# Stick-breaking attention with two heads per step and running sums over later keys, and one block of the top-k selection moved into attention A

## What is computed

```python
# branch B: stick-breaking attention, 8 heads of width 64, strictly causal
z = einsum('bqhd,bkhd->bhqk', q, k) * D_B ** -0.5
strict = k_pos[None, :] < q_pos[:, None]
log_beta = log_sigmoid(z)
log_keep = where(strict, log_sigmoid(-z), 0.0)
log_stick = cumsum(log_keep, axis=3, reverse=True) - log_keep   # over later keys
a = where(strict, exp(log_beta + log_stick), 0.0)
out = einsum('bhqk,bkhd->bqhd', a, v)

# branch C: the indexer's scores choose the top 128 keys of each query
score = einsum('bqhk,bqh->bqk', relu(qi . ki), wi)
_, sel = top_k(score, kk)          # then softmax attention over the selected keys
```

## Time and profile before

| | us |
|---|---|
| median of 3 runs | 3432.1 (3431.77 to 3432.5) |
| the profiled execution | 3431.2 |
| its span in the trace | 3429.4 |
| TensorE busy | 3248.8 (95%) |
| VectorE busy | 1513.7 (44%) |
| GpSimd busy | 1065.1 (31%) |
| ScalarE busy | 979.2 (29%) |

### The profile page before, as it was taken

How to read it: one execution, slowest core, us unless ns; L and a number is a source line. 1 busy time by engine, 2 the same in 40 slices (tenths; PEclk the granted TensorE clock), 3 DMA queues, 4 the chain that set the end, 5 groups by cost and what they waited for, 6 DMA issues and landing times.

```text
span 3429.4 us, 54570 instructions
## 1 busy us (share of the span) xinstructions
PE 3248.8 (95%) x23070; PEld 2941.3 (86%) x23070; DVE 1513.7 (44%) x1869; ACT 979.2 (29%) x1647; POOL 1065.1 (31%) x499
## 2 busy tenths in 40 slices
PE   8999979899999998999999998897999999899997
PEld 7999978846777998999899998787567779899997
DVE  4553234820335436553265533167113354465532
ACT  3222223262223223222232222232522232322221
POOL 3334333301222333334334433332021223334442
PEclk9999989988999999999999999998989999999998
DMA  6221232201111132222212212221010112222221
GB/s 168 86 86 68 104 104 79 75 7 42 49 38 59 65 113 70 90 82 76 100 62 87 89 68 93 98 103 58 1 62 29 47 58 78 103 74 86 78 85 60
DMA packets 43105, 255.51 MB, mean 75 GB/s; under 512 B 6048, under 2 KB 6144, under 8 KB 26048
## 3 DMA queue, kind: packets, MB, share of 16 engines
q1 hardware_dynamic: 37008, 235.64, 19.3%
q0 software_dynamic: 5840, 17.50, 1.9%
q10 hardware_dynamic: 96, 0.08, 0.0%
HBM read 237.34 MB, written 15.85 MB: 74 GB/s over the span
## 4 chain that ended last, share of the span: by engine, by line
PE 86%; DVE 10%; issue 2%; ACT 1%; DMA 0%; DVEq 0%; SPq 0%; ACTq 0%
PE PS L597 33%; PE PS L602 16%; PE PS L833 12%; PE PS L994 2%; PE PS L560 2%; DVE arena L1608 2%; DVE m L1606 2%; PE PS L710 2%; DVE rstd L1413 2%; PE PS L572 2%; PE PS L619 2%; PE PS L947 1%; PE PS L945 1%; PE PS L844 1%; PE PS L802 1%
## 5 line engine op out<-in xcount | busy, mean ns | idle before, releaser
L401 POOL TENSOR_TENSOR ring_r<-ring,piece_h 128x1024 fp32r<-128x1024 f32 (+1 forms) x240 | 630.5, 2629 | 1020.9 <-ACT piece_h L1079 1020.9
L401 POOL TENSOR_TENSOR ring_r<-ring,piece_m 128x1024 fp32r<-128x1024 f32 (+1 forms) x172 | 364.8, 2126 | 961.6 <-ACT piece_m L1079 961.4
L1079 ACT ACTIVATE piece_h<-ring 128x1024 fp32r<-128x1024 f32 (+1 forms) x240 | 274.6, 1146 | 1147.6 <-PE PS L602 1138.6
L597 PE MATMUL PS<-uT_r,piece_h 128*128 128x272 f32 x2688 | 555.0, 287 | 6.1 <-DVE sq L1493 6.1
L597 PE MATMUL PS<-u_l,piece_h 128*128 128x272 f32 x2688 | 554.9, 288 | 0.0
L602 PE MATMUL PS<-uT_r,ring_r 128*128 128x272 f32 x3328 | 449.9, 287 | 0.0
L602 PEld LDWEIGHTS PS<-uT_r,ring_r 128*128 128x128 f32 x3328 | 429.6, 188 | 0.0
L597 PEld LDWEIGHTS PS<-uT_r,piece_h 128*128 128x128 f32 x2688 | 421.7, 188 | 7.0 <-ACT piece_h L1079 7.0
L597 PEld LDWEIGHTS PS<-u_l,piece_h 128*128 128x128 f32 x2688 | 419.3, 188 | 0.0
L597 PE MATMUL PS<-act_l,piece_h 128*128 128x272 f32 x1408 | 292.1, 289 | 0.0
L597 PE MATMUL PS<-act_h,piece_h 128*128 128x272 f32 x1408 | 291.4, 288 | 0.0
(11 more groups left out here) (242 smaller groups left out, 4979.5 us busy)
## 6 DMA issues: line engine op xcount, KB each, us to landing
ring<-in_w_up SPq DMA_DIRECT2D x88, 1024.0 KB, 4.8
ring<-in_w_dn SPq DMA_DIRECT2D x64, 704.0 KB, 4.2
ring<-in_w_mg SPq DMA_DIRECT2D x48, 768.0 KB, 4.3
ring<-in_w_in SPq DMA_DIRECT2D x24, 1024.0 KB, 4.7
ring<-in_w_out SPq DMA_DIRECT2D x8, 1024.0 KB, 4.8
x_spill<-xT SPq DMA_DIRECT2D x2, 2176.0 KB, 8.8
xT<-x_spill SPq DMA_DIRECT2D x2, 2176.0 KB, 8.7
ring<-in_w_vb SPq DMA_DIRECT2D x4, 1024.0 KB, 4.7
```

What stands on the lines that cost most here:

```text
L401: nc.gpsimd.tensor_tensor(ring_r[:, ch[0] % NSLOT, at:at + n], w, hi, ALU.subtract).then_inc(S["w_low"], 1)
L597: mm(PS[:, 2 * u + b, 0:HALF], w, x[k][:, HALF * b:HALF * b + HALF], start=first and k == 0 and n == 0, stop=False)
L1079: A(buf[:, hs, 0:n], ring[:, ch % NSLOT, at:at + n], ACT.Copy).then_inc(S["w_high"], 1)
```

## The change

- **Tile order.** `kr`, `krs`, `ql` and `kv` come directly behind `qC`; `qB` and `kB` come last. The sums of squares of `kv` are taken after the tiles `qB0` and `qB1`, in banks 6 and 7, with their root in a place of its own (`rstd_kv`). ACT's waits for `lat_ready` and `sel_ready` ahead of branch B go.
- **Memory.** `acc`, `topw`, `eqv`, `cum` and `rel` of the selection move into `xT`.
- **Selection.** DVE does the blocks s = 1 and 2, then the rotation and the latents, then s = 4, and enters branch B. The 16 rounds of s = 3 (512 keys) are done one per unit in units 2 to 17 of attention A, and the final eight operations behind unit 18.
- **Branch B.** A step `u` is a pair of heads and one block of keys, 16 steps for the prompt and three more, in the same loop, for the new tokens. A pair uses two neighbouring banks out of three pairs of banks (0, 2, 6), so that `scores(u)` waits for the weights of step u-3. All ACT and DVE operations of a step are twice as wide. DVE keeps a running sum of the softplus of all later blocks (`later_keys`, two additions per pair of heads), and `cumulate` multiplies it with `neg_ones` once. `values(u)` is called in every step, the two heads into the two halves of the PSUM partitions. The waits for ACT's weights, `sb_a_ready` and `sb_pv`, start from 3 and 1.
- **GpSimd.** The rows of `kB` are written out behind those of `kr` and `ckv`.

The core of the diff:

```diff
 UNITS = [(p, s, e) for p in range(4) for s in range(NBLK) for e in range(2)] + [(4, 4, 0), (4, 4, 1)]
 N_UNIT = 2 * len(UNITS)
 N_PAIR = 10
-N_B = H * NBLK
+N_HP = 4
+N_BP = N_HP * NBLK
+N_BU = N_BP + 3
 MASK_AT = [0, 128, 384, 768, 1280]
 MASK_W = [128, 256, 384, 512, W_S]
-ACC_AT = {1: 0, 2: 256, 3: 640, 4: 1152}
+ACC_AT = {1: 1024, 2: 1280, 4: 1664, 3: 2176}
 
 
 def mixer_tiles():
 
     t = ["kI"] + [f"qI{i}" for i in range(4)] + ["kC", "vw", "v0", "v1"]
-    t += [f"qC{i}" for i in range(4)] + [f"qB{i}" for i in range(4)] + [f"kB{i}" for i in range(4)]
-    t += ["kr", "krs"] + [f"ql{i}" for i in range(KQ)] + [f"kv{i}" for i in range(KKV)]
+    t += [f"qC{i}" for i in range(4)] + ["kr", "krs"] + [f"ql{i}" for i in range(KQ)] + [f"kv{i}" for i in range(KKV)]
...
+        def later_keys(i):
+
+            return sb_s[:, :, (128, 1024, 1280)[i - 1]:(256, 1280, 1664)[i - 1]]
+
+        def stick_weights(u):
+
+            i = u % 4
+            at = P * (i * (i + 1) // 2)
+            return sb_a[:, :, at:at + P * (i + 1)] if u < N_BP else sb_a[:, :, P * (u - N_BP):P * (u - N_BP) + P]
...
@@ -735,9 +759,9 @@
                     split_tile(name, u_h, u_lo, IN_PIECES[i][0], IN_PIECES[i][1])
                     if name in ("ql1", "ql2", "kv0"):
                         square_sum(l, "q", ("ql1", "ql2", "kv0").index(name))
-                for k in range(KKV):
-                    square_sum(l, "kv", k)
-                for name in ("kv0", "kv1"):
+                    if name in ("qB0", "qB1"):
+                        square_sum(l, "kv", ("qB0", "qB1").index(name))
+                for name in ("kB2", "kB3"):
                     pe.wait_ge(vacated[TILE[name] % 2], l * T_LAYER + turn_of(name) + 3)
                 branch_b(l)
...
+                def scores(u):
+                    bank = pair_bank(u)
+                    pe.wait_ge(S["sb_a_ready"], nb + u + 1)
+                    if u < N_BP:
+                        hp, j = u // 4, 3 - u % 4
+                        w = SEQ - P * j
+                        for e in range(2):
+                            mm(PS[:, bank + e, 0:w], kB[64 * e:64 * e + 64, hp, P * j:P * j + P], qB[64 * e:64 * e + 64, hp, P * j:SEQ],
+                               start=True, stop=False, skip_group_check=True)
+                        if u == 0:
+                            pe.wait_ge(S["masks_ready"], l * 3 + 3)
+                        for e in range(2):
+                            ins = mm(PS[:, bank + e, 0:P], ident_r[:], sb_mask_r[:], start=False, stop=True, skip_group_check=True)
...
+                def cumulate(u):
+                    bank = pair_bank(u)
+                    pe.wait_ge(S["sb_sp_ready"], nb + u + 1)
+                    if u < N_BP:
+                        i = u % 4
+                        w = P * (i + 1)
+                        if i >= 2:
+                            pe.wait_ge(S["sb_later"], l * 2 * N_HP + 2 * (u // 4) + i - 1)
+                        for e in range(2):
+                            if i:
+                                mm(PS[:, bank + e, P:w], neg_ones, later_keys(i)[:, e, :], start=False, stop=False, skip_group_check=True)
+                            ins = mm(PS[:, bank + e, 0:w], neg_tri, soft_plus(u)[:, e, :], start=False, stop=True, skip_group_check=True)
...
+                def values(u):
+                    hp, i = u // 4, u % 4
+                    j = 3 - i
+                    pe.wait_ge(S["sb_a_ready"], nb + u + 4)
+                    if i == 0 and hp >= 2:
+                        pe.wait_ge(S["sb_out"], l * 5 + hp - 1)
+                    for e in range(2):
+                        h = 2 * hp + e
+                        ins = mm(PS[64 * e:64 * e + 64, 4 + hp % 2, P * j:SEQ], VB[:, j, DH * h:DH * h + DH], stick_weights(u)[:, e, :],
+                                 start=i == 0, stop=i == 3, skip_group_check=True)
                     ins.then_inc(S["sb_pv"], 1)
...
+                for v in range(N_BU + 3):
+                    if v < N_BU:
+                        scores(v)
+                    if 0 <= v - 2 < N_BU:
+                        cumulate(v - 2)
+                    if 0 <= v - 3 < N_BP:
+                        values(v - 3)
...
-                    to_queries(f"qB{i}", qB[:, i, :], scale=DH ** -0.5)
-                for i in range(4):
-                    to_keys(f"kB{i}", kB[:, i, :])
-                act.wait_ge(S["idx_acc"], l * 32 + 34)
                 to_queries("kr", kr_raw[:, 0, :])
                 to_queries("krs", kr_raw[:, 1, :])
                 for i in range(KQ):
                     u = evac(f"ql{i}")
                     square(l, "q", i, unit(u)[:, :, 0:HALF])
                     to_queries(f"ql{i}", ql[:, i, :], at_hand=True)
-                root(l, "q")
                 for i in range(KKV):
                     u = evac(f"kv{i}")
                     square(l, "kv", i, unit(u)[:, :, 0:HALF])
                     to_keys(f"kv{i}", ckv[:, i, :], at_hand=True)
-                act.wait_ge(S["lat_ready"], l * 7 + 3)
-                root(l, "kv")
-                act.wait_ge(S["sel_ready"], l * 4 + 4)
-                act.wait_ge(S["idx_done"], l * 32 + 32)
+                root(l, "q")
+                for i in range(4):
+                    to_queries(f"qB{i}", qB[:, i, :], scale=DH ** -0.5)
+                    if i == 2:
+                        act.wait_ge(S["idx_acc"], l * 32 + 34)
+                        root(l, "kv", rstd_kv, 6)
+                for i in range(4):
+                    to_keys(f"kB{i}", kB[:, i, :])
                 act.wait_ge(S["rows_ki"], 16 * (l * 2 + 2))
                 branch_b(l)
...
@@ -1534,19 +1549,20 @@
 
                 link(l, V.memset(msk[:, 0:P], 0.0))
                 link(l, V.memset(msk[0:CHUNK, CHUNK:P], -BIG))
-                for s in range(1, 5):
-                    select(l, s)
+                select(l, 1, 1)
+                select(l, 2, 2)
                 rotate_keys(l)
 
                 invert(l, "q")
                 for k in range(KQ):
                     V.scalar_tensor_tensor(out=ql[:, k, :], in0=ql[:, k, :], scalar=g_of(l, 24 + k), in1=rstd[:],
                                            op0=ALU.mult, op1=ALU.mult).then_inc(S["lat_ready"], 1)
-                invert(l, "kv")
+                invert(l, "kv", rstd_kv)
                 for k in range(KKV):
                     for a, b, c in ((0, SEQ, 0), (KEY_NEW, NKEY, SEQ)):
                         V.scalar_tensor_tensor(out=ckv[:, k, a:b], in0=ckv[:, k, a:b], scalar=g_of(l, 27 + k),
-                                               in1=rstd[:, c:c + b - a], op0=ALU.mult, op1=ALU.mult).then_inc(S["lat_ready"], 1)
+                                               in1=rstd_kv[:, c:c + b - a], op0=ALU.mult, op1=ALU.mult).then_inc(S["lat_ready"], 1)
+                select(l, 4, 3)
                 dve.wait_ge(S["rows_ki"], 16 * (l * 2 + 2))
                 branch_b(l)
                 dve.wait_ge(S["rows_out"], 16 * (l * 12 + 12))
...
                 dve.wait_ge(S["merge_ready"], l * KD + n + 1)
 
-            def select(l, s):
+            def select_round(l, s, r):
+
+                w, k = MASK_W[s], (TOPK if s < 4 else TOPK_S)
+                src = acc[:, ACC_AT[s]:ACC_AT[s] + w] if r == 0 else topw[:, 0:w]
+                link(l, V.max(m8[:], src))
+                if r < k // 8 - 1:
+                    link(l, V.match_replace(topw[:, 0:w], m8[:], src, LOWEST))
+
+            def select(l, s, n):
+                for r in range((TOPK if s < 4 else TOPK_S) // 8):
+                    select_round(l, s, r)
+                select_last(l, s, n)
+
+            def select_last(l, s, n):
+
...
+                rows = (NEW, P, P)
+                for at in (0, 896):
+                    ins = V.memset(sb_s[:, :, at:at + P], 0.0)
+                link(l, ins)
+                for u in range(N_BU):
+                    m, w = (P, P * (u % 4 + 1)) if u < N_BP else (rows[u - N_BP], P)
+                    dve.wait_ge(S["sb_soft"], nb + u + 1)
+                    if u >= 3:
+                        dve.wait_ge(S["sb_cum"], nb + (u - 2 if u < N_BP else N_BP - 1))
+                    if u >= 4:
+                        dve.wait_ge(S["sb_later"], l * 2 * N_HP + 2 * (u // 4) if u < N_BP else (l + 1) * 2 * N_HP)
+                    V.scalar_tensor_tensor(out=soft_plus(u)[0:m], in0=PS[0:m, pair_bank(u):pair_bank(u) + 2, 0:w], scalar=0.0,
+                                           in1=sb_e[u % 2][0:m, :, 0:w], op0=ALU.max, op1=ALU.add).then_inc(S["sb_sp_ready"], 1)
+                    if u < N_BP and u % 4 in (1, 2):
+
+                        before = sb_s[:, :, 0:256] if u % 4 == 1 else sb_s[:, :, 896:1280]
+                        n = l * 2 * N_HP + 2 * (u // 4) + u % 4
+                        dve.wait_ge(S["sb_sp_ready"], nb + u + 1)
+                        if u % 4 == 2:
+                            dve.wait_ge(S["sb_later"], n - 1)
```

(5 more changed lines are left out.)

## The result

The changed kernel takes 3376.8 us (median of 4 runs, 3372.3 to 3380.8), the kernel before 3431.9 beside it (3431.0 to 3432.5): ratio 0.9839, 95% interval 0.9822 to 0.9856. The profiled execution has a span of 3374.7 us against 3429.4, 54.7 less.

| layer 0 | before, us | after, us | difference | predicted |
|---|---|---|---|---|
| first scores of branch B | 669.5 | 670.4 | +0.9 | +1.3 |
| branch B to the next tile | 132.9 | 99.1 | -33.8 | -30.9 |
| from there to the first maximum of attention A | 48.9 | 50.0 | +1.1 | 0 |
| attention A, first to last maximum | 144.7 | 147.3 | +2.6 | +1.5 |
| sum | | | -29.2 | -28.1 |

The account below looks back on a forecast made before the run. TensorE was taken as the bound, with a stall on VectorE before branch B. Per layer 39.6 us gained, less 10 for clock and 1.5 for selection, gives 28.1, twice 56: 3376 us, range 3350 to 3403.

Parts of the forecast that it names:

- The stall: Before branch B's first softplus: TensorE's 18.38 us wait for VectorE disappears, with its 13.1 us at half clock.
- TensorE work of 14.9 us per pair: Branch B: TensorE's own work per pair of heads falls from 21.6 to 14.9 us, 17.2 at worst.
- The half that no row showed: Branch B: `values` of two heads in two halves of the output partitions saves nothing to 2.3 us; 2.3 taken.
- The chain through ScalarE: Branch B: next scores wait for weights behind ScalarE's three passes; 18.8 us per pair, TensorE idle about 4.
- The clock: Branch B: 30 us per layer at half clock cost 10 us, bounds 0 and 20.
- the slower rival: Half clock through all of branch B because of waits in each step: 3454 us, chance 0.07.
- the prediction's rival: Latents or their roots reach VectorE late, branch B still waits; 25 us per layer return: 3426 us, chance 0.04.
- 12.4 us of filling: Start of branch B: the first four steps fill the pipeline in 12.4 us.
- Selection in attention A: Attention A: moved rounds cost nothing, the last eight operations 0 to 5 us per layer, 1.5 taken.
- The clock did not stay up: Rival for branch B: the clock stays up, each layer gains 38 to 40 us: 3353 us, chance 0.19.
- Scores that don't pair: Rival in branch B: two heads' scores don't run together, 16 us for both layers: 3393 us, chance 0.06.
- VectorE as the bound of attention A: Rival in attention A: half of the moved 33.6 us per layer shows: 3407 us, chance 0.10.

Follow-up runs that it names:

- the spread version: Changed kernel with the last eight operations of the moved block spread over units 18 to 24 of attention A: 3365.4 us, 3368.0 on another chip.

## Why the prediction was right, point by point

- **The stall (18.38 us and 13.1 at half clock) goes.** Right. VectorE was to be ready at 656.7; it was at 665.8, 9 us later: the first two blocks ended 2.2 us later than in the kernel before (629.8, not 627.6), VectorE waited 3.57 us for the root of `kv`, and two groups of operations took 3.8 us more than the same ones in the version with the block put back (L1563 3.88 against 1.74 us, L1634 2.05 against 0.37). Both ran beside a GpSimd operation (646.67 to 649.16 and 658.69 to 661.09), which they had none of there. Of the 13 us to spare 7.19 were left. The first scores came at 670.40 (670.8 predicted).
- **TensorE work of 14.9 us per pair.** 16.29 with the dip in it, 14.53 at full clock in the version with the weights first. The half that no row showed, `values` in column halves, holds: 1.08 us for both heads. The Trainium skill's statement (TensorE: Matmul & The Clock Gate, Part 3: Packing small matmuls) that column groups run at the same time agrees with it.
- **The chain through ScalarE, steps of 4.0, 5.3, 4.2 and 5.25 us.** Measured at full clock 3.96, 5.25, 4.20 and 5.28, together 18.69 (18.8 predicted). That it is this chain and not TensorE was shown by changing ScalarE's order alone. TensorE waits 4.10 us per pair (4 predicted).
- **The clock.** 30 us at half clock that cost 10 were predicted, 24.7 were there. Three dips cost 1.7 each, the first (6.47 us from 677.48 to 683.95 instead of 5.28) 1.2, and the last at least 1.8: the thin products at the end take 7.35 us in it, and 5.51 with the block put back, where only their second part is at half clock. No run shows its whole price. That is 8 us or somewhat more. The 28 us that the prediction took for a pair at half clock stand in no row; twice its 14.9 is 29.8, with which its term would be 11. The size was near; its form was not foreseen: I took it as a lump, and it is a dip about once per pair, tied to the two waits. The rule that the prediction cited (the Trainium skill, TensorE: Matmul & The Clock Gate, "A second HAM failure mode: psum-queue depth-cycling"), a clock that goes up and down through short idles between groups, is what the traces show, but at one dip of 3.4 us in a pair of 20.4, and the slower rival, half clock all through, stayed away.
- **What each part brings.** The sum put 1.8 us per pair on the running sums. They save them in TensorE's work, and the clock takes most of it back: 2.3 us for both layers in branch B, 1.3 in the end. The stall with its half clock stood for 25 us per layer in the prediction's rival; putting the block back costs 10.2, since the wait at the pipeline's start, ScalarE's first passes and a dip take its place, and attention A gets some back. The sum had them as 12.4 us of filling, so it came out right where the single price would not have.
- **Selection in attention A at 1.5 us per layer.** 1.4 us without a dip, 2.6 and 7.4 with one. The rounds cost nothing, as said. The term lacked the clock: behind TensorE's wait of 0.7 to 0.9 us came up to 13.7 us at half clock.
- **The rivals.** The clock did not stay up in the changed kernel; its dips within the pairs went only with one more edit (useless products, the weights first, or no running sums), and at branch B's end it fell in every version. Scores that don't pair were priced at 16 us and would have cost 36. VectorE as the bound of attention A and the stall staying did not come.
- **Luck.** That the forecast of 3376 is met within 1 us is partly luck. In layer 0 branch B was put 2.9 us too long and the other three rows together 1.8 us too short, and layer 1 with the rest of the span lost 25.5 us where 28.1 were forecast.

What stays open is the width of the changed kernel's runs: attention A's dips can explain a part of it and the length of branch B's last dip another, but the runs of the spread version differ by 2.9 to 4.8 us, and with one trace for each measurement the whole width can't be put down to them. Why the same wait is followed by a dip in one execution and by none in another is open too.

## What to carry to other kernels

When a chain of several engines takes over from TensorE as the bound, look first at the order on the engine in the middle: the operation that frees a buffer belongs ahead of the ones that fill the next, and moving two lines here brought 39 us, beside the 54 of the whole change. Work taken off TensorE while it waits for others is worth little, above all where the longer waits go with a lower clock (1.3 us here, and about 6 once the weights came first), so read the granted clock step by step and not as a mean. Work moved into another engine's idle time goes in pieces no longer than that idle time.

## What the runs showed of the hardware

- TensorE's clock fell for 3.4 us once per pair after waits of 1.42 and 2.04 us with 3.2 us of work between them (717.74 to 720.97), and not after the same waits when products on zeros took up 0.9 and 1.5 us of them, nor in the version without running sums, which has the same two waits and 1.7 us more work in the two steps behind them. What decides between these was not tried further.
- The same wait of TensorE in attention A, 0.7 to 0.9 us, was followed in different executions by no dip, by 3.4 us and by 13.7 us at half clock.
- Two fp32 products of 64 rows for the two halves of the rows, as neighbours, take 1.06 us for 512 columns (717.74 to 718.80), apart 1.06 each with a mask product between: 3.5 us per pair of heads in all.
- A VectorE addition of two SBUF operands of 128 columns, 0.29 us elsewhere, took 4.82 us where it began 0.2 us after a GpSimd operation of 4.87 us (2659.74 to 2664.61), and ended 0.15 us after it. In the version without running sums and with the spread it began 0.15 us ahead of that operation (2653.05 and 2653.20) and took 0.29 us.
